# A quarter-size last level in three triangular inverses, and another order of the splits at two seams

## The reference

```
x = x + [forgetting attention | mLSTM] @ w_out          # projections by w_in ("win")
x = x + peer_ffn(rmsnorm(x))                            # 16384 experts, top 16 x 8 heads
h = x + [gated delta rule | RWKV-7] @ w_out_2           # "dn", "rw", "out2"
h = h + cross_attention(rmsnorm(h), rmsnorm(mem))
h = h + squared_relu_mlp(rmsnorm(h))                    # "ffn", hidden 8192
out = rmsnorm(h)
```

## Time and profile before

| | us |
|---|---|
| median of 3 runs | 4068.8 |
| lowest and highest | 4067.99, 4075.9 |
| the profiled execution, its own time | 4068.18 |
| its span in the profile | 4066.4 |

### The profile page before, as it was taken

The page is one execution under the profiler, slowest core; times in us unless marked ns, Lnnn a source line. Parts: engine busy times, 40 slices in busy tenths (PEclk is TensorE's granted clock), DMA queues, the critical chain, the costliest instruction groups (busy, mean ns, idle before and its releaser), DMA issues.

```text
span 4066.4 us, 54872 instructions
## 1 busy us (share of the span) xinstructions
PE 3741.2 (92%) x22490; PEld 3333.6 (82%) x22490; DVE 2466.1 (61%) x2662; ACT 1491.9 (37%) x1256; POOL 190.3 (5%) x174
## 2 busy tenths in 40 slices
PE   8996899999999999999999998858777979999998
PEld 7985799999988888888889997847667867888887
DVE  3544548977677766666666633576665446566666
ACT  3333333345443333333344333222222333333333
POOL 1000000000000000000000000413121000000000
PEclk8998999999999999999999998988787989999999
DMA  4551445556677756556654542010102424555554
GB/s 169 172 190 51 154 158 182 197 197 228 249 237 242 261 199 210 196 197 203 203 191 156 169 174 83 0 52 0 42 21 88 171 94 166 192 189 186 191 190 145
DMA packets 122888, 650.34 MB, mean 160 GB/s; under 512 B 10736, under 2 KB 43888, under 8 KB 49552
## 3 DMA queue, kind: packets, MB, share of 16 engines
q1 hardware_dynamic: 116224, 620.20, 44.0%
q0 software_dynamic: 6544, 28.44, 1.9%
HBM read 620.81 MB, written 27.79 MB: 160 GB/s over the span
## 4 chain that ended last, share of the span: by engine, by line
PE 85%; DVE 10%; ACT 2%; issue 1%; DMA 1%; POOL 0%; DVEq 0%; ACTq 0%; SPq 0%; PEldq 0%
PE pairs L2247 18%; PE pairs L2248 18%; PE pairs L2249 18%; PE quad L2292 12%; PE quad L2293 6%; DVE w_low L1994 2%; PE quad L2403 2%; PE pairs L2405 2%; PE quad L2395 1%; PE quad L2333 1%; PE quad L2766 1%; DVE arena L1895 0%; ACT w_high L1101 0%; PE quad L2689 0%; PE quad L2690 0%
## 5 line engine op out<-in xcount | busy, mean ns | idle before, releaser
L1994 DVE TENSOR_TENSOR w_low<-ring,w_high 128x2048 fp32r<-128x2048 f32 (+1 forms) x547 | 1252.8, 2291 | 932.0 <-ACT w_high L1101 931.5
L1101 ACT CAST w_high<-ring 128x2048 fp32r<-128x2048 f32 (+1 forms) x547 | 1039.4, 1901 | 1749.0 <-PE pairs L2249 1280.1
L2247 PE MATMUL pairs<-x_t,w_high 128*128 128x256 f32 x2592 | 744.6, 287 | 21.9 <-DVE w_low L1994 14.1
L2248 PE MATMUL pairs<-x_t,w_high 128*128 128x256 f32 x2592 | 738.0, 285 | 0.0
L2249 PE MATMUL pairs<-x_t,w_low 128*128 128x256 f32 x2592 | 737.8, 285 | 0.0
L2292 PE MATMUL quad<-x_t,w_high 128*128 128x512 f32 x1984 | 705.9, 400 | 13.6 <-DVE w_low L1994 13.6
L2247 PE MATMUL pairs<-w_high,act_high 128*128 128x512 f32 x1568 | 612.9, 391 | 10.2 <-DVE w_low L1994 6.5
L2248 PE MATMUL pairs<-w_low,act_high 128*128 128x512 f32 x1568 | 612.2, 390 | 0.0
L2249 PE MATMUL pairs<-w_high,act_low 128*128 128x512 f32 x1568 | 611.7, 390 | 0.0
L2293 PE MATMUL quad<-x_t,w_low 128*128 128x256 f32 x1984 | 558.9, 282 | 0.0
L2247 PEld LDWEIGHTS pairs<-x_t,w_high 128*128 128x128 f32 x2592 | 502.3, 194 | 24.8 <-DVE w_low L1994 16.8
(11 more groups left out here) (523 smaller groups left out, 3616.0 us busy)
## 6 DMA issues: line engine op xcount, KB each, us to landing
ring<-pu SPq DMA_DIRECT2D x128, 1024.0 KB, 4.9
ring<-pv SPq DMA_DIRECT2D x128, 1024.0 KB, 4.9
ring<-f SPq DMA_DIRECT2D x128, 1024.0 KB, 4.7
ring<-win SPq DMA_DIRECT2D x48, 1024.0 KB, 4.9
ring<-dn SPq DMA_DIRECT2D x32, 1024.0 KB, 4.9
ring<-rw SPq DMA_DIRECT2D x24, 1024.0 KB, 4.7
ring<-wout SPq DMA_DIRECT2D x16, 1024.0 KB, 4.8
ring<-wq SPq DMA_DIRECT2D x16, 1024.0 KB, 4.8
```

Of the source, the lines that this page charges most:

```text
L1101: nc.scalar.copy(WH[s % 2][:, 0:w], flat(ring[s])[:, 0:w]).then_inc(ev["split_high"], 1)
L1994: v.tensor_tensor(WL[s % 2][:, 0:w], flat(ring[s])[:, 0:w], WH[s % 2][:, 0:w].bitcast(F32), ALU.subtract).then_inc(ev["split_low"], 1)
L2247: mm(out, stat[0], mov[0], start=start, stop=False, skip_group_check=True)
L2248: mm(out, stat[0], mov[1], start=False, stop=False, skip_group_check=True)
```

## The change

In each inverse the loop now ends after level 5. Level 6 is written out behind it and works on 64x64 blocks: with T11 and T22 the two inverted diagonal blocks and A21 the block below the diagonal, the only new part is -T22 A21 T11, and only its transpose is made. TensorE multiplies from a 64-row, 64-column quadrant of the array into the other half of the partitions: 4 products of 64x64 by 64 columns for M1, 4 for the transposed result, and none for T itself. A^T is read directly, so GpSimd makes no mask product in this level. ScalarE copies 64 partitions by 256 elements in place of 128 by 512, and VectorE writes the negated 64 by 256 block in place of two 128x512 subtractions. The counts of `inv_off` are 20 per inverse in place of 24; the others stay.

At the win seam ScalarE's order goes from highs 0, highs 1, rows 0-7 to highs 0, rows 0-3, highs 1, rows 4-7, and VectorE's from rows 0-3, lows 0, lows 1, rows 4-7 to lows 0, rows 0-3, lows 1, rows 4-7. At the ffn seam VectorE's goes from rows 0-7, lows 1 to rows 0-3, lows 1, rows 4-7; ScalarE's stays.

```diff
 def inverse_pool(pool, c, At):
-            for l in range(1, 7):
+            for l in range(1, 6):
 def inverse_act(act, c):
-            with act.Fori(1, 7, 1) as l:
+            with act.Fori(1, 6, 1) as l:
                 for q in range(4):
...
+            for q in range(4):
+                g = 24 * c + 20 + q
+                act.wait_ge(ev["inv_m1"], g + 3)
+                act.wait_ge(ev["inv_t"], g + 1)
+                nc.scalar.copy(M1B[64:P, q % 2, :, 0:64], PQ[64:P, q % 2, 0:256].rearrange("p (m j) -> p m j", m=4)
+                               ).then_inc(ev["inv_m1_out"], 1)
 # ScalarE, start of win
-            highs("win", 0, (0, 1))
-            rows(0, range(8))
+            highs("win", 0, (0,))
+            rows(0, range(4))
+            highs("win", 0, (1,))
+            rows(0, range(4, 8))
 def inverse_dve(dve, o, v, c, A, At, Ti, Tt, ready):
-            with dve.Fori(1, 7, 1) as l:
+            with dve.Fori(1, 6, 1) as l:
...
+            for q in range(4):
+                dve.wait_ge(ev["inv_t"], 24 * c + 20 + q + 3)
+                v.tensor_scalar(Tt[0:64, 4 * q:4 * q + 4, 64:P], PP[0:64, q % 2, 0, 0:256].rearrange("p (m j) -> p m j", m=4),
+                                -1.0, None, ALU.mult).then_inc(ev["inv_new"], 1)
 # VectorE, start of ffn
-            rows(6, range(8))
+            rows(6, range(4))
             lows("ffn", 0, (1,))
+            rows(6, range(4, 8))
 # VectorE, start of win
+            lows("win", 0, (0,))
             rows(0, range(4))
-            lows("win", 0, (0, 1))
+            lows("win", 0, (1,))
             rows(0, range(4, 8))
-        def inverse_pe(pe, mm, c, Ti, Tt):
+        def inverse_pe(pe, mm, c, At, Ti, Tt):
-            with pe.Fori(1, 7, 1) as l:
+            with pe.Fori(1, 6, 1) as l:
                 def first(q):
-                    pe.wait_ge(ev["inv_off"], g + 1)
+                    pe.wait_ge(ev["inv_off"], 4 * l + (20 * c - 3 + q))
...
+            def last_first(q):
+                g = 24 * c + 20 + q
+                pe.wait_ge(ev["inv_new"], 28 * c + 21 + q)
+                pe.wait_ge(ev["inv_m1_out"], g + 1)
+                for m in range(4):
+                    ins = mm(PQ[64:P, q % 2, m * 64:(m + 1) * 64], At[0:64, 4 * q + m, 64:P], Ti[0:64, 4 * q + m, 0:64],
+                             start=True, stop=True)
+                ins.then_inc(ev["inv_m1"], 1)
+
+            def last_then(q):
+                pe.wait_ge(ev["inv_m1_out"], 24 * c + 20 + q + 3)
+                pe.wait_ge(ev["inv_new"], 28 * c + 20 + q + 3)
+                for m in range(4):
+                    ins = mm(PP[0:64, q % 2, 0, m * 64:(m + 1) * 64], M1B[64:P, q % 2, m, 0:64], Tt[64:P, 4 * q + m, 64:P],
+                             start=True, stop=True)
+                ins.then_inc(ev["inv_t"], 1)
+            # last_first 0, 1; last_then 0; last_first 2; last_then 1; last_first 3; last_then 2, 3
```

More of the change, by code:

```diff
@@ L2414, in inverse_pe @@
                 then(3)
+            def last_first(q):
[13 more added lines that the diff above has]
+                ins.then_inc(ev["inv_t"], 1)
+            last_first(0)
+            last_first(1)
+            last_then(0)
+            last_first(2)
+            last_then(1)
+            last_first(3)
+            last_then(2)
+            last_then(3)
         def stage2_pe(pe, mm, product, turn, turn_into, turned_rows, ready):
@@ L2495, in stage2_pe @@
             pe.wait_ge(*nth("v_tok", 4))
-            inverse_pe(pe, mm, 0, TI, TTI)
+            inverse_pe(pe, mm, 0, AT_, TI, TTI)
             at = lambda b, h: PQ[:, b + h // 4, (h % 4) * P:(h % 4 + 1) * P]
@@ L2665, in rw_pe @@
                 ins.then_inc(ev["ram_turned"], 1)
-            inverse_pe(pe, mm, 1 + hf, RTI, RTT)
+            inverse_pe(pe, mm, 1 + hf, GR[:, :, 0, :], RTI, RTT)
             pe.wait_ge(ev["inv_new"], 28 * (hf + 2))
```

## The result

The kernel after takes 4034.4 us (median of 4 runs, 4031.4 to 4034.82) against 4069.2 for the kernel before (4067.99 to 4075.9): a ratio of 0.9908, with a 95% interval from 0.9893 to 0.9923, 34.8 us less. The forecast was 4035.0, with 4028 to 4053 around it. The profiled execution took 4034.49 us, with a span of 4032.6.

A forecast was written before the change was run, and what follows sets the result against it. TensorE was taken as the bound, busy 92% of the span and 85% of the chain. Inverses 21.6, win seam 6.2 and ffn seam 5.5 sum to 33.3 us, taking 4068.2 to 4035 us, range 4028 to 4053.

The forecast's parts named there:

- The last level's cadence: Last level of each inverse: 64x64 loads with 64-column matmuls start 0.054 us apart, 0.43 us per group.
- Rival 1: Last level: small matmuls stay at the full ones' 0.11 us cadence; 4.5 us saved each, 4043 us in all; chance 0.17.
- rival 2: Last level: load and matmul in one quadrant don't overlap, 0.35 us each; slower than before, 4089 us; chance 0.07.
- copy 0: Last level: ScalarE's copy following the first group of first products, forecast at 0.90-1.27 us from the first issue.
- T0: Last level: first group of transposed (second) products, forecast at 1.32-1.75 us from the first issue.
- F2, T1, F3, T2: Last level: groups of first (F) and second, transposed (T) products, forecast one behind another from 1.75 to 3.47 us.
- The change of shape: Last level: 0.2 us until TensorE's array has changed shape, taken once.
- Behind inverse 2: VectorE's queued subtraction for out2's slot 0 delays the step that TensorE's next product waits for: 0.8 us lost.
- The win seam: Subtraction for slot 0 moves ahead of the rows, removing TensorE's 3.69 us gap and shortening slot 0: 6.2 us.
- the clock term: Win seam: without the pause slot 0 takes 5.76 us, not 8.31, at the higher clock: another 2.55 us.
- The ffn seam: VectorE's earlier subtraction for slot 1 removes TensorE's 3.69 us wait, plus 1.8 us of lower clock: 5.5 us.
- Rivals 3 and 4: 3: clock falls in last level, 4053 us, chance 0.10; 4: low tail clock comes back earlier, 4028 us, chance 0.05.

The follow-up runs named there:

- e6: Kernel after with waits added so a group of first products never runs beside a group of transposed ones; 4042.86 us, ratio 0.9933.
- v8: Kernel after with VectorE's subtraction for out2's slot 0 moved behind the first time step after inverse 2; 4031.38 us in one execution.
- e1: Kernel after with the seams' order of before, so the new last level alone; 4045.56 us, ratio 0.9938.
- e7: Kernel before with 16 extra, unread program products between the first row products and slot 0 of win; 4068.82 us, ratio 0.9998.
- e2: Kernel before with the new order at both seams, inverses as before; 4058.32 us, ratio 0.9972.
- e3: Kernel before with the new order at the win seam alone; 4063.81 us, ratio 0.9989.
- v9: The kernel after with out2's slot 0 subtraction moved later, plus levels 2 to 5's products each split into two diagonal 64x64 quadrants; 3974.51 us, ratio 0.9764.

## Why the prediction was right

- **The last level's cadence.** Taken as 0.054 from the nearest row, measured 0.058, so a group takes 0.47 us for the forecast's 0.43. Rival 1 (0.11) and rival 2 (0.35) would have shown at once in the starts; both fell. Rival 2 was the rule, taken alone, of the Trainium skill ("TensorE: Matmul & The Clock Gate", Part 3) that a weight load overlaps matmuls in flight only when the row group differs. The trace disagrees for this kernel: loads into one and the same quadrant start 0.058 us apart while the matmuls last 0.22, and the measurement decides.
- **The shape of the level.** From the first matmul on, the forecast had copy 0 at 0.70 us, T0 at 1.12 and the last write at 4.23 (each less the 0.20 that it put ahead). Measured: 0.71, 1.13, and 3.84. The step that was mis-sized is the one that ran the groups F2, T1, F3, T2 one behind another at 0.43 us each. First and transposed products use different quadrants and run side by side: T0, F2, T1 and F3 are issued in 1.38 us. The forecast had read two halves of the array at once out of L2657's rows, but did not ask whether its own groups could do it. The level was 0.4 us shorter for it; e6, which forbids it, takes 1.74 us more, most of that for its waits and for the clock. The change of shape is there as forecast, but ahead of the level: 3037.73 is the last full-size matmul, and the first small one starts 0.2 us behind it. Net of the 0.1 by which that exceeds the usual spacing, 8.0 us went in each level, 24 for a forecast of 22.4.
- **The copy and the write.** ScalarE's copy lasted 0.37 us, forecast 0.365; VectorE's write 0.417, forecast 0.42.
- **Behind inverse 2.** The loss is 0.88 us for a forecast of 0.8, and v8 removes exactly it.
- **The inverses together.** 24 - 0.9 = 23.1 for a forecast of 21.6; e1 alone gives 23.5.
- **The win seam.** The pause is gone and slot 0 takes 5.84: 3.69 + 0.25 + (8.31 - 5.84) = 6.4 us for a forecast of 6.2, and 0.5 more from the row products ahead of it, which is chance. e7 shows that the clock term has its cause in the pause; the second profile of before shows that its size is not fixed, 7.31 - 5.84 = 1.5 us there and 2.5 in the first. In the kernel after part of the lead goes again: it is 6.9 us, 5.3 by 80 us and 4.7 by 422 us. That is no price of the new order: e2, with the same seam, keeps its lead (6.2 and 6.3), e3's grows from 7.5 to 9.3, and e1, with the old seam, loses the same 1.5 us by 80 us.
- **The ffn seam.** 5.6 us in the two casts around it, forecast 5.5, with the clock at 1.00 in every profile without the pause.
- **The sum.** The terms were 21.6 and 6.2 + 5.5 = 11.7; by the parts run alone they are 23.5 and 10.8. So the inverses were priced 1.9 us too low and the seams 0.9 too high, and the whole change is worth 34.8 us for a forecast of 33.3. The forecast was counted down from the profiled execution, which lay 1.0 us under the median of before, and so only 0.6 of the 1.5 us shows in the time. That it came so close is partly luck: single executions of the kernel before lie up to 8 us apart (4067.99 to 4075.9).
- **Rivals 3 and 4**, both on the clock. It is 1.00 in all three last levels, so rival 3 fell in its place; it was not far off, since in e6 the same matmuls with waits between them end at 0.55 to 0.72. Nor did a tail gain 7 us by an earlier rise. What the clock did between the inverses, which the forecast said it could not work out, moved mile posts by up to 3 us within one kernel. From inverse 0's last update to inverse 1's first matmul the four profiles with the new level and nothing else changed there (both of the kernel after, e1, v8) take 135.5 us, the six with the old level 131.9 to 135.2. Whether a part of that is a price of the new level stays open.

## What to carry to other kernels

Where an operand has zero quadrants or only one output quadrant is wanted, cut the product to 64x64 blocks: the load and the stream both shrink, and groups that use different quadrants run at the same time if the queue puts them next to each other with nothing to wait for between them. When TensorE gets faster, read what stands in the other engines' queues ahead of the step that it waits for next; a long operation that used to fit beside the product is then on the path (0.88 us here, cured by one moved line). Price a pause of TensorE by its length and by what the clock does behind it, but claim only what the place itself shows: a gain of 2 or 3 us in one profile is no gain of the kernel until repeated runs show it.

## What the runs showed of the hardware

- Two 64x64 quadrants work at the same time, both on the two diagonal quadrants (v9, 0.029 us for each fp32 hardware matmul of 64 columns with its load) and on the two off the diagonal (the kernel after, L2435 and L2443 started together at 2630.10 and 2630.16). In one quadrant it is 0.058 us.
- A group that must wait for the group before it in another quadrant starts 0.73 us behind that one's start in place of 0.47, with 0.20 us of idle loading (e6).
- After a pause of 3.7 to 4.0 us of TensorE the granted clock over the next slot was 0.66 to 0.77, in all four profiles with it at the win seam and in all five at the ffn seam; without it, or with 0.78 us left of it (e7), it was 1.00.
- The two profiles of the kernel after agree within 0.9 us all along, those of the kernel before differ by up to 3.1 us in one stage and meet again within 0.4 at the end. The stage's clock was 0.78 once and 0.74 once. What decides between the two was not found.
